# Residual sums between the halves of a weight tile's low part, and the attention's normalisation moved from VectorE to ScalarE

## What is computed

```python
for l in range(DEPTH):                       # DEPTH = 2
    x = x + 0.5 * _swiglu(_rms_norm(x, norm_ffn1[l]), ffn1_w_gate[l], ffn1_w_up[l], ffn1_w_down[l])
    h = _rms_norm(x, norm_mix[l])
    proj = (h @ w_in[l]).astype(jnp.float32)
    p_rwkv = _token_shift(proj[..., :D_SHIFT], shift_mu[l])
    y_rwkv = _rwkv7_mixer(p_rwkv, ...)       # 6 heads of 64: a linear recurrence over the tokens
    y_attn = _attention_mixer(proj[..., D_SHIFT:D_SHIFT + 3 * D_ATTN], ...)   # 6 heads, softmax over 256 keys
    y_conv = _conv_mixer(proj[..., D_SHIFT + 3 * D_ATTN:], ...)               # 31 taps, 256 channels
    mix = jnp.concatenate([y_rwkv, y_attn, y_conv], axis=-1)
    x = x + mix @ w_out[l]
    x = x + 0.5 * _swiglu(_rms_norm(x, norm_ffn2[l]), ffn2_w_gate[l], ffn2_w_up[l], ffn2_w_down[l])
```

## Time and profile before

| | us |
|---|---|
| runs: median (lowest to highest of 3) | 1374.80 (1374.46 to 1376.41) |
| the profiled execution's own time | 1374.69 |
| its span in the profile | 1372.6 |
| TensorE busy (share of the span) | 1342.7 (98%) |
| weight loads, beside the matmuls | 1162.9 (85%) |
| VectorE | 976.1 (71%) |
| ScalarE | 742.5 (54%) |
| GpSimd | 154.2 (11%) |

### The profile page before, as it was taken

The page is one execution under the profiler, slowest core; times in us unless marked ns, Lnnn a source line. Parts: engine busy times, 40 slices in busy tenths (PEclk is TensorE's granted clock), DMA queues, the critical chain, the costliest instruction groups (busy, mean ns, idle before and its releaser), DMA issues.

```text
span 1372.6 us, 24759 instructions
## 1 busy us (share of the span) xinstructions
PE 1342.7 (98%) x9701; PEld 1162.9 (85%) x9701; DVE 976.1 (71%) x1310; ACT 742.5 (54%) x1050; POOL 154.2 (11%) x154
## 2 busy tenths in 40 slices
PE   9999999999999999999999999999999999999997
PEld 7888889977788888888887987788888997788885
DVE  6666666678776666766657766886666766998787
ACT  6444456566744445644447656564444545655553
POOL 3000000097000000000000049300000033000000
PEclk9999999999999999999999999999999999999999
DMA  9856355023476535755529121465663952456530
GB/s 338 268 187 196 111 178 175 32 95 110 165 244 195 198 123 185 264 188 183 183 68 297 57 93 34 145 225 186 187 200 102 303 184 98 153 186 217 197 134 31
DMA packets 170483, 230.57 MB, mean 168 GB/s; under 512 B 4687, under 2 KB 151815, under 8 KB 170149
## 3 DMA queue, kind: packets, MB, share of 16 engines
q1 hardware_dynamic: 167920, 223.75, 49.9%
q10 hardware_dynamic: 1877, 5.59, 1.1%
q0 software_dynamic: 608, 0.12, 0.1%
HBM read 228.39 MB, written 2.63 MB: 168 GB/s over the span
## 4 chain that ended last, share of the span: by engine, by line
PE 88%; DVE 5%; ACT 4%; issue 1%; POOL 1%; DMA 1%; SPq 0%; POOLq 0%; DVEq 0%; ACTq 0%
PE banks L490 37%; PE banks L658 27%; PE banks L662 14%; PE banks L1548 1%; DVE up_lo L475 1%; DMA w_up<-in_ffn_w_up_dram 1%; DVE gate_lo L475 1%; ACT up_hi L470 1%; ACT gate_hi L470 1%; PE banks L1333 1%; PE banks L1190 1%; PE banks L613 0%; PE banks L941 0%; PE banks L1180 0%; DVE x L856 0%
## 5 line engine op out<-in xcount | busy, mean ns | idle before, releaser
L658 PE MATMUL banks<-hT,up_hi 128*128 128x512 f32 x880 | 220.8, 393 | 0.0
L475 DVE TENSOR_TENSOR down_lo<-w_down,down_hi 128x2048 fp32r<-128x2048 f32 (+1 forms) x65 | 147.8, 2274 | 93.4 <-ACT down_hi L470 93.4
L737 ACT ACTIVATE work<-banks 128x256 f32<-128x256 f32 x176 | 66.9, 384 | 258.3 <-PE banks L662 257.8
L658 PE MATMUL banks<-hT,gate_hi 128*128 128x512 f32 x800 | 199.7, 392 | 0.1
L470 ACT ACTIVATE down_hi<-w_down 128x2048 fp32r<-128x2048 f32 (+1 forms) x65 | 123.7, 1903 | 115.9 <-PE banks L490 115.9
L658 PEld LDWEIGHTS banks<-hT,up_hi 128*128 128x128 f32 x880 | 158.2, 189 | 29.2 <-issue 0.6
L475 DVE TENSOR_TENSOR up_lo<-w_up,up_hi 128x2048 fp32r<-128x2048 f32 x72 | 164.7, 2287 | 15.9 <-ACT up_hi L470 15.8
L475 DVE TENSOR_TENSOR gate_lo<-w_gate,gate_hi 128x2048 fp32r<-128x2048 f32 x64 | 146.9, 2296 | 37.2 <-ACT gate_hi L470 37.1
L658 PEld LDWEIGHTS banks<-hT,gate_hi 128*128 128x128 f32 x800 | 146.9, 188 | 28.8 <-DVE gate_lo L475 0.5
L490 PE MATMUL banks<-down_hi,ff_hi 128*128 128x512 f32 x400 | 156.2, 391 | 0.0
L490 PE MATMUL banks<-down_lo,ff_hi 128*128 128x512 f32 x400 | 156.2, 391 | 0.0
(11 more groups left out here) (390 smaller groups left out, 2200.1 us busy)
## 6 DMA issues: line engine op xcount, KB each, us to landing
w_up<-in_ffn_w_up_dram SPq DMA_DIRECT2D x44, 1024.0 KB, 5.4
w_down<-in_ffn_w_down_dram SPq DMA_DIRECT2D x44, 1024.0 KB, 5.2
w_gate<-in_ffn_w_gate_dram SPq DMA_DIRECT2D x43, 1024.0 KB, 5.4
w_up<-in_w_in_dram SPq DMA_DIRECT2D x12, 1024.0 KB, 9.6
w_gate<-in_w_up_dram SPq DMA_DIRECT2D x11, 1024.0 KB, 5.1
w_up<-in_w_up_dram SPq DMA_DIRECT2D x11, 1024.0 KB, 5.1
w_down<-in_w_down_dram SPq DMA_DIRECT2D x11, 1024.0 KB, 5.0
w_down<-in_w_in_dram SPq DMA_DIRECT2D x9, 1024.0 KB, 8.5
```

Source lines behind the costliest of these rows:

```text
L475: dve.tensor_tensor(staged[kind][1][:, 0:cols], slot[sl][:, 0:cols], staged[kind][0][:, 0:cols].bitcast(F32), ALU.subtract).then_inc(split ...
L658: pe.matmul(bank[:, :], w[0][:, c, at], hpair[:, :, c, :], start=c == 0, stop=False)
L737: act.activation(to[:, q, j * SEQ:(j + 1) * SEQ], psum[2 * q + j][:, SEQ:], ACT.Copy)\
```

## The change

1. **Seam before the second feed-forward.** VectorE's order becomes: residual sum 0, the first half (columns 0 to 1023) of `gate0`'s low part, residual sums 1 and 2, the second half, then low parts of chunks 0 and 1, and the rest as before. ScalarE's small `Sqrt` moves from behind the high part of `gate0` to ahead of it (and ahead of the seven DMAs in the second layer). `dve_raw` and `act_raw` keep the old lines for the other seam alone (n = 0).
2. **Normalisation.** `normalise(h)` in the chain becomes `invert(h)` on VectorE (the reciprocal alone, semaphore `sum_inverted`) and `normalise(h)` on ScalarE (two copies with a scale per row). VectorE inverts for head 0 ahead of the chain and for heads 1 to 5 in groups 0, 4, 6, 10, 12; ScalarE normalises in groups 0, 1, 4, 6, 10, 12, in a group behind the chain's copies, `copy`, other turned tiles and `prior_values`, and ahead of `exps`, `out_`, the high part of the `w_out` tile and `act_mixed`.
3. **First step.** Its second product `E2T` goes from kind "copy" (ScalarE) to "move" (VectorE), for both batches.
4. **Semaphores.** Several that are used once or twice in a layer are merged (`kk_sum`, `qk_sum` and `gn_var` into `head_sum`, and so on), with counts to match. The order of the instructions isn't touched by it.

```diff
@@ chain_plan
-        [("copy", "E2", "DT", "D"), ("copy", "E2T", "D", "DT")],
+        [("copy", "E2", "DT", "D"), ("move", "E2T", "D", "DT")],
@@ act_raw
-            act.activation(unused, eps["norm"], ACT.Sqrt)
+            if n == 0:
+                act.activation(unused, eps["norm"], ACT.Sqrt)
@@ dve_raw
-            dve_residual(dve, uses, kind, n - 1, COLUMNS, range(3), mixed=n > 0)
+            if n == 0:
+                dve_residual(dve, uses, kind, n - 1, COLUMNS, range(3))
@@ DveAttention
+            def invert(self, h):
+                self.dve.wait_ge(S["exp_done"], 2 * h + 2 + past["exp_done"])
+                self.dve.reciprocal(arec[:, h, :], asum[:, h, :]).then_inc(S["sum_inverted"], 1)
@@ ActAttention
+            def normalise(self, h):
+                self.act.wait_ge(S["sum_inverted"], h + 1 + past["sum_inverted"])
+                for t, (lo, hi) in enumerate(((0, P), (P, 3 * P))):
+                    row = self.logit[:, h % 2, lo:hi]
+                    ins = self.act.activation(row, row, ACT.Copy, scale=arec[:, h, t:t + 1])
+                ins.then_inc(S["p_ready"], 1)
@@ pe_mix (one of the merged semaphores)
-            head_sums(pe, psum[3], lambda c, t: bonus[:, c, tokens(t)]).then_inc(S["kk_sum"], 1)
+            head_sums(pe, psum[3], lambda c, t: bonus[:, c, tokens(t)]).then_inc(S["head_sum"], 1)
...
@@ act_mix, in the loop over the groups i
+                if i in (0, 1, 4, 6, 10, 12):
+                    attention.normalise((0, 1, 4, 6, 10, 12).index(i))
                 if i in (0, 3, 5, 9, 11):
                     attention.exps((0, 3, 5, 9, 11).index(i) + 1)
@@ dve_mix
-            attention.normalise(0)
-            attention.normalise(1)
+            attention.invert(0)
             for i, (step, b) in enumerate(GROUPS_OF_CHAIN):
...
-                if i in (4, 6, 10, 12):
-                    attention.normalise((4, 6, 10, 12).index(i) + 2)
+                if i in (0, 4, 6, 10, 12):
+                    attention.invert((0, 4, 6, 10, 12).index(i) + 1)
@@ vector engine, in the loop over the layers
                 dve_mix(dve, uses, link)
-                dve_ahead(dve, uses, ("gate0",))
+                dve_residual(dve, uses, "down", 1, COLUMNS, (0,), mixed=True)
+                dve.wait_ge(high["gate0"], uses.now("gate0"))
+                for at in (slice(0, 1024), slice(1024, 2048)):
+                    ins = dve.tensor_tensor(staged["gate"][1][:, at], slot["gate0"][:, at],
+                                            staged["gate"][0][:, at].bitcast(F32), ALU.subtract)
+                    if at.start == 0:
+                        dve_residual(dve, uses, "down", 1, COLUMNS, (1, 2), mixed=True)
+                ins.then_inc(split["gate0"], 1)
                 dve_raw(dve, uses, 2, "norm_ffn2", "down", link)
```

More of the change, by code:

```diff
@@ L170 @@
 SIGNALS = {
+    "head_sum": 4, "head_root": 4, "head_inv": 2, "head_rows": 2, "head_spread": 4, "keys_ready": 2, "cl_stat": 2,
     "gain_ready": 1, "rows_picked": 2, "params_psum": 2, "params_ready": 1,
@@ L1444, in pe_mix @@
                                       kkrows[:, 3 * t + c, :], ident)
-            mm.then_inc(S["kk_spread"], 1)
+            mm.then_inc(S["head_spread"], 1)
             pe_tile(pe, uses, 6, n_norm)
@@ L1468, in pe_mix @@
             pe_tile(pe, uses, 9, n_norm, (0,))
-            qk_sums(1).then_inc(S["qk_sum"], 1)
+            qk_sums(1).then_inc(S["head_sum"], 1)
             pe_tile(pe, uses, 9, n_norm, (1,))
@@ L1494, in pe_mix @@
             pe_values_tile(pe, uses, 10)
-            pe.wait_ge(S["k_rows"], 1 + past["k_rows"])
+            pe.wait_ge(S["head_rows"], 2 + past["head_rows"])
             pe.wait_ge(S["v_centred"], 1 + past["v_centred"])
@@ L1505, in pe_mix @@
             turn(2)
-            pe.wait_ge(S["k_ready"], 1 + past["k_ready"])
+            pe.wait_ge(S["keys_ready"], 2 + past["keys_ready"])
             turn(3)
@@ L1690, in pe_mix @@
                 mm = pe.matmul(psum[0][:, 0:SEQ], ones, mix[:, 6 + c, :], start=(c == 0), stop=(c == 1))
-            mm.then_inc(S["cl_mean"], 1)
+            mm.then_inc(S["cl_stat"], 1)
             gn_spread(0)
@@ L1700, in pe_mix @@
                 mm = pe.matmul(psum[1][:, 0:SEQ], ones, proj[:, CG + c, 1:], start=(c == 0), stop=(c == 1))
-            mm.then_inc(S["cl_var"], 1)
+            mm.then_inc(S["cl_stat"], 1)
             out_ready(1, 4)
@@ L1766, in act_mix @@
             high(6)
-            act.wait_ge(S["kk_sum"], 1 + past["kk_sum"])
-            act.activation(kkst, psum[3][:, 0:12], ACT.Sqrt, bias=eps["kk"]).then_inc(S["kk_root"], 1)
+            act.wait_ge(S["head_sum"], 1 + past["head_sum"])
+            act.activation(kkst, psum[3][:, 0:12], ACT.Sqrt, bias=eps["kk"]).then_inc(S["head_root"], 1)
             shift(4)
-            act.wait_ge(S["kk_inv"], 1 + past["kk_inv"])
-            act.activation(by_head(kkrows), over_heads(kkst, 12), ACT.Copy).then_inc(S["kk_rows"], 1)
+            act.wait_ge(S["head_inv"], 1 + past["head_inv"])
+            act.activation(by_head(kkrows), over_heads(kkst, 12), ACT.Copy).then_inc(S["head_rows"], 1)
             high(7)
@@ L1786, in act_mix @@
             copy(8)
-            act.wait_ge(S["qk_sum"], 1 + past["qk_sum"])
-            act.activation(qkst, psum[3][:, 0:24], ACT.Sqrt, bias=eps["norm"], scale=1.0 / 64).then_inc(S["qk_root"], 1)
-            act.wait_ge(S["qk_inv"], 1 + past["qk_inv"])
-            act.activation(by_head(krows_), over_heads(qkst[:, 12:24], 12), ACT.Copy).then_inc(S["k_rows"], 1)
+            act.wait_ge(S["head_sum"], 2 + past["head_sum"])
+            act.activation(qkst, psum[3][:, 0:24], ACT.Sqrt, bias=eps["norm"], scale=1.0 / 64).then_inc(S["head_root"], 1)
+            act.wait_ge(S["head_inv"], 2 + past["head_inv"])
+            act.activation(by_head(krows_), over_heads(qkst[:, 12:24], 12), ACT.Copy).then_inc(S["head_rows"], 1)
             copy(9)
@@ L1883, in act_mix @@
             for k in range(2):
-                act.wait_ge(S["gn_var"], k + 1 + past["gn_var"])
+                act.wait_ge(S["head_sum"], k + 3 + past["head_sum"])
                 act.activation(gnst[:, 6 * k:6 * k + 6], psum[4 + k][:, 0:6], ACT.Sqrt, bias=eps["gn"], scale=1.0 / 64)\
-                   .then_inc(S["gn_root"], 1)
+                   .then_inc(S["head_root"], 1)
             act_high(act, uses, OUT_SLOTS[2], kind=OUT_KINDS[2])
@@ L1893, in act_mix @@
                    .then_inc(S["mix_high"], 1)
-            act.wait_ge(S["cl_var"], 1 + past["cl_var"])
+            act.wait_ge(S["cl_stat"], 2 + past["cl_stat"])
             act.activation(proj[:, CG, 1:], psum[1][:, 0:SEQ], ACT.Sqrt, bias=eps["ln"], scale=1.0 / 256)\
@@ L1940, in dve_mix @@
             low(6)
-            dve.wait_ge(S["kk_root"], 1 + past["kk_root"])
-            dve.reciprocal(kkst, kkst).then_inc(S["kk_inv"], 1)
+            dve.wait_ge(S["head_root"], 1 + past["head_root"])
+            dve.reciprocal(kkst, kkst).then_inc(S["head_inv"], 1)
             dve.wait_ge(S["iclr_sig"], 3 + past["iclr_sig"])
@@ L1949, in dve_mix @@
             low(7)
-            dve.wait_ge(S["kk_spread"], 1 + past["kk_spread"])
+            dve.wait_ge(S["head_spread"], 1 + past["head_spread"])
             for v, at in three(6):
                 ins = dve.tensor_tensor(kk[:, at, :], kk[:, at, :], v, mult)
-            ins.then_inc(S["kk_ready"], 1)
-            dve.wait_ge(S["kk_ready"], 1 + past["kk_ready"])
+            ins.then_inc(S["keys_ready"], 1)
+            dve.wait_ge(S["keys_ready"], 1 + past["keys_ready"])
             link(dve.tensor_tensor(bh, kk, bh, mult))
@@ L2008, in dve_mix @@
             below(1)
-            dve.wait_ge(S["qk_root"], 1 + past["qk_root"])
+            dve.wait_ge(S["head_root"], 2 + past["head_root"])
             link(dve.reciprocal(qkst, qkst))
-            dve.tensor_scalar(qkst[:, 0:12], qkst[:, 0:12], 0.125, None, mult).then_inc(S["qk_inv"], 1)
+            dve.tensor_scalar(qkst[:, 0:12], qkst[:, 0:12], 0.125, None, mult).then_inc(S["head_inv"], 1)
             mats_of(0)
```

44 lines of the change are left out of this document (22 added, 22 removed).

## The result

| | before | after |
|---|---|---|
| median of 20 runs, us (lowest to highest) | 1375.08 (1374.33 to 1377.37) | 1378.33 (1374.71 to 1386.28) |
| ratio to the runs of before, 95% interval | | 1.0024 (1.0016 to 1.0033) |
| profiled execution: own time / span, us | 1374.69 / 1372.6 | 1383.61 / 1381.5 |
| its mean granted clock | 0.998 | 0.991 |

The change made the kernel slower, by about 3 us. The forecast of 1375.3 us is under that, and the highest time of its range, 1377.6, too. What strikes first is the spread. Eight of the 20 runs after lie at 1374.7 to 1375.6 with a mean clock of 0.997 to 0.998, the other twelve at 1377.7 to 1386.3 with 0.988 to 0.996: the lower the mean clock, the longer the run. Before, all 20 lie within 3.1 us.

The account below looks back on a forecast made before the run. TensorE is busy for 1342.7 of 1372.6 us, so only its gaps can be won. The seam's -3.0 and the chain's +3.5 give +0.5 on 1374.69, forecast 1375.3 us, range 1372.0 to 1377.6.

Parts of the forecast that it names:

- Part 1: Seam before the second feed-forward: TensorE's 1.51 us wait for residual sums goes in each layer, 3.0 us won.
- The Trainium skill's drain: Seam: by the skill's page, 1.38 us beside the table load would cut the win by 0.3 to 0.4 a layer; not counted.
- The price of ScalarE's pair: Chain: two scaled copies normalising a head hold ScalarE for 0.69 us and are ready after 0.79.
- Group 6: Chain, head 3: the pair ahead of `out_(0)` delays TensorE's turn, +0.69 us in the first layer, +0.4 in the second.
- Groups 10 to 12: Chain, heads 4 and 5: the pairs delay ScalarE's later copies, +1.25 us in the first layer, +1.2 in the second.
- the 1.0 that was named as a sign: Chain: the high part of the `w_out` tile would start about 1.0 us later than before against its group.
- The last wait: Chain's last step: TensorE's wait for ScalarE's copy would grow from 0.36 to some 0.8 to 1.6 us.
- Part 3: Start of the chain: moving the `E2T` copies to VectorE costs nothing, between -0.2 and +0.4 us.
- The sum: Whole kernel: 3.0 us won at the seam, 3.5 lost in the chain, +0.5 on 1374.69, giving 1375.3 us.
- The rivals: Faster: the chain takes it, about 1372.0 and under, chance 0.22. Slower: the seam gives nothing, 1378.3, chance 0.18.
- B: Seam gives nothing: the gate product's opening waits for the second half and chunk 0; 1378.3 us, chance 0.18.
- less than 2.7 us: Whole kernel: a difference under 0.2% of the time was held to be indistinguishable from no change.

Follow-up runs that it names:

- the seam alone: The kernel before with the seam's new order and merged semaphores only, E2T and all normalisations as before: median 1372.55 us, lowest 1371.04, ratio 0.9981.
- heads 0 to 2: The changed kernel with heads 3, 4 and 5 normalised on VectorE again, E2T still on VectorE: median 1371.92 us, ratio 0.9977, none of 11 fallen.
- the kernel with its gaps filled: The changed kernel plus 2, 1, 3 and 1 unused products in TensorE's four chain gaps: median 1375.22 us, ratio 0.9999, none of 11 fallen.
- chain alone: The kernel before with normalisation on ScalarE, E2T on VectorE and merged semaphores, the seam as before: median 1383.23 us, ratio 1.0054, 6 runs.
- heads 4 and 5: The kernel before plus the new seam, with only heads 4 and 5 normalised on ScalarE, E2T as before: median 1378.61 us, ratio 1.0017, eight of 12 fallen.
- head 4 alone: The kernel before plus the new seam, with only head 4 normalised on ScalarE: median 1376.89 us, ratio 1.0008, eight of 12 fallen.
- Head 5 alone: The kernel before plus the new seam, with only head 5 normalised on ScalarE: median 1372.46 us, ratio 0.9978, none of 11 fallen.
- the gap of 0.99 filled: New seam, only head 4 normalised on ScalarE, plus three unused products in TensorE's 0.99 us gap: median 1372.69 us, ratio 0.9986, none of 11 fallen.

## Why the prediction was wrong, step by step

- **Part 1.** Right, in mechanism and size: 2.96 us by the lowest runs for 3.0, the wait of the turns gone, the gate product opened in time. The seven DMA issues cost nothing either: in the seam alone, second layer, they are issued from 880.05 on beside the table load (880.69, 1.28 long), and the high part follows at 882.80.
- **The Trainium skill's drain** of about 1.38 us behind a table load ("ScalarE: Activation LUTs", "What ACT_TABLE_LOAD costs") did not show here either: the load ends at 354.53, the small `Sqrt` is at 354.55 to 354.75, and the high part starts at 355.39, where it had to wait for TensorE anyway. By the drain, an estimate from that section's figures (353.25 + 2.66 + 0.20), it could not have started before 356.1.
- **The price of ScalarE's pair.** Right: 0.79 to 0.80 until it is done, the next instruction 0.69 to 0.70 after its start (300.64 to 301.33, 308.03 to 308.73), for 0.79 and 0.69.
- **Group 6.** Right: +0.69 and +0.43 for +0.69 and +0.4. That the first agrees to the hundredth is luck, since the stretch itself differs by 0.17 between two kernels with the same chain.
- **Groups 10 to 12.** Right: +1.25 and +1.19 for +1.25 and +1.2. The high part of the `w_out` tile starts 1.75 behind `values(1)` (308.73 and 306.98) where it started 0.71 behind it (306.61 and 305.90), the 1.0 that was named as a sign. The last wait was 0.85, in the forecast's 0.8 to 1.6; ahead of it stood another of 0.99, which the sum holds but which the forecast didn't name.
- **Part 3.** Right in the change as made, but half of its reason wasn't seen: it is free because head 1's normalisation leaves VectorE's queue at the same time. Alone it costs 4.8 us by the medians. With heads 0 to 2 it wins 0.7, more than the 0.2 that was allowed.
- **The sum.** 1375.3 was the time of the eight runs after whose clock stayed up (1374.7 to 1375.6), and of the kernel with its gaps filled (1375.22). By the parts that kernel has -3.0 + 3.2 = +0.2 for the forecast's +0.5, the chain's 3.2 being inside the bounds of 2.4 and 4.2.
- **The step that failed** is that the sum has no term for TensorE's clock. The working says that more work on a busy engine "moves the end one for one" and takes this for the whole price, and behind the chain it counts on "its own work without long gaps" at full speed; the term for the clock is nothing, without a reason, in the sum, in the range and in both rivals. The waits did cost one for one. On top of that 12 of 20 runs lie 3.0 to 11.6 us over the lowest, and in the profiled one 20.5 us behind the two chains ran at half the clock. The forecast had listed all the gaps and had added them up as time; it hadn't asked how much TensorE would work between them. In 310 to 315 that fell from 4.41 to 3.16 us.
- **The rivals.** Neither of the two came true. B named the measured time to the tenth (1378.3), by luck: its mechanism, a seam that gives nothing, did not happen. The remark that less than 2.7 us can't be told from no change was not what decided: the 3.3 us measured are clear of the noise with 20 runs (1.0016 to 1.0033).

Open: why the clock falls behind the same gaps in some executions and not in others, or in one layer and not in the other of the same execution; whether it is the idle time or the small products around it; and what brings the short falls near 338.

## What to carry to other kernels

Count TensorE's gaps twice: once as time, and once as what they may do to the clock, since here a cluster of gaps of under 1 us each was followed by 7 to 14 us at half the clock, in some executions and not in others. So a single run, or a sum made on one, doesn't show it: look at the spread of the runs beside their mean clock. Where a later chain must keep such a gap, a product that nothing needs and that fits into it can be worth its place: three of them turned eight fallen runs of 12 into none of 11. Not to open the gap is simpler: the kernel with the lowest times here leaves heads 3 to 5 on VectorE. And when work is moved off an engine together with other work onto it, ask whether each half is free alone: the copies of `E2T` were only because of the move beside them.

## What the runs showed of the hardware

- The granted clock fell to 0.50 behind stretches in which TensorE never stood idle for more than 0.99 us at a time, but was busy for only 3.15 to 3.16 of 5 us (after, chain alone, heads 4 and 5). Behind the same gaps it stayed at 1.00 in other layers of the profiles (3.15 in the chain alone, first layer; 3.06 in heads 4 and 5, second layer), and behind 3.54 (head 4 alone) as well. Head 5 alone, with 3.92 in its profile, had none of 11 runs fallen.
- It also fell where TensorE had been busy for 4.89 of 5 us (at 337.9, with the gap of 0.99 filled), for 3.4 us.
- A fall lasted 6.8 us in one place and 13.7 in the other of the same execution, 6.8 in the chain alone and 10.2 in heads 4 and 5. TensorE was busy throughout all four.
- A float32 product of 128 x 128 x 128 costs TensorE about 0.25 us when several stand in a row (eight in 1.98), and appears as two matmul records. In a gap its cost is nothing as long as the row of them ends before the wait does.
